# Hybrid encoder layer on one core: activations become the stationary matmul operand, split weights stream past them 512 columns at a time

## The chip, the cores and the metric

One core of a Trainium2 chip runs the whole program in one launch. The metric is the device time of that launch in microseconds. Before the change it is 2490.61 us, the median of 3 runs (2490.39 to 2492.17). Everything is float32 in HBM.

## What is computed

256 tokens of width 2048 go through one encoder layer. Cut to what matters:

```python
x = x + 0.5 * swiglu_ffn(rms_norm(x), w_gate, w_up, w_down)     # 2048 -> 5632 -> 2048
h = rms_norm(x)
u = h @ w_in          # conv a, conv gate (2048 each), q latent 768, kv latent 512, k rope 64, two gates of 2048
y_conv = silu(layer_norm(depthwise_conv31(a * sigmoid(gate)) + b)) @ w_pw_out
y_mla  = attention(16 heads: q from (rms_norm(c_q) @ w_uq), k and v from (rms_norm(c_kv) @ w_ukv), rope) @ w_o
x = x + (sigmoid(gl_conv) * y_conv + sigmoid(gl_mla) * y_mla) @ w_out
x = x + 0.5 * swiglu_ffn(rms_norm(x), w_gate2, w_up2, w_down2)
return rms_norm(x)
```

The weights are read once from HBM (427 MB read over the span). With 256 tokens the arithmetic lies almost wholly in the products with weights.

## The kernel before

**Split products.** A float32 product is made of three passes in the type fp32r: each weight tile is rounded by ACT into `w_hi` (`round_unit`, line 332, a Copy), DVE writes the remainder `w_lo = raw - w_hi` (`split_unit`, line 780), and the activations are kept as a rounded half and a remainder too (`h`, `hidden`, `attn`, `merged`, `c_q`, `c_kv`: 256 columns of high part and 256 of low part for each tile of 128 channels). `multiply` issues the three matmuls:

```python
pe.matmul(dst[:, 0:T], w_hi[:, j, rows], moving[:, 0:T], start=start, stop=False)      # line 554
pe.matmul(dst[:, 0:T], w_hi[:, j, rows], moving[:, T:2 * T], start=False, stop=False)  # line 555
pe.matmul(dst[:, 0:T], w_lo[:, j, rows], moving[:, 0:T], start=False, stop=stop)       # line 556
```

The first operand after the destination is the stationary one: a 128x128 tile of weights is loaded into the array (LDWEIGHTS), and all 256 tokens (`T`) stream past it. So a result has channels on partitions and tokens along the row, which is the form in which the next product wants it.

**Units and slots.** The weights come as a stream of 760 units through four slots. SP's queue loads `raw[:, j]` once `lo_ready` tells that DVE is done with the slot (line 275), ACT rounds it once PE has used the slot four units earlier (`unit_used`), DVE splits it, PE multiplies. A unit is 128x1024 (8 weight tiles, 24 matmuls), in the two `down` stages 128x1408 (11 tiles, 33 matmuls), in two units of each head pair 128x1152.

**Stages**, in the order of PE's queue: ffn1_up, ffn1_down, conv_in, latents, heads (8 pairs), mla_out, conv_gate, conv_out, w_out, ffn2_up, ffn2_down. `over` makes hardware loops of equal groups. PE accumulates in two banks in turn and waits in `wait_bank` until DVE has read one (`tile_read`). DVE's and ACT's queues are written out by hand between the splits and roundings: `times` (line 814) reads a bank and applies the norm's factor, which lies along the tokens, `absorb` (lines 824 to 832) squares, rounds and splits a new tile of `x`, ACT takes the silu and the sigmoids (line 376, 385). The sums of squares are added tile by tile on DVE and summed over partitions by a matmul with ones (line 614), for which PE waits at the start of a stage. The convolution's 31 taps for each of 16 channel tiles run on DVE alone (`convolve`, line 958: one 128x256 instruction for each tap and tile), spread over conv_in, heads and mla_out. In heads, the scores (lines 670, 671), the transposes of the probabilities (line 679) and the product with the values (line 688) are full float32, and the rope swap is a matmul (line 727).

Of the kernel before, what the change touches and what calls it, by code (L numbers as in the profile page):

```python
# [14 lines left out]
P = 128  # L31
# [5 lines left out]
N_HEADS = 16  # L37
ROPE = 64
# [9 lines left out]
SLOTS = 4  # L48
UNIT_MAX = FT // 4


PHASES = [
    ("ffn1_up", FT, (8, 8, 8, 8), 2),
    ("ffn1_down", KT, (FT // 4,) * 4, 1),
    ("conv_in", KT, (8, 8, 8, 8), 2),
    ("latents", 6, (8, 8, 8, 8), 2),
    ("heads", N_HEADS // 2, (9, 9, 8, 8), 6),
    ("mla_out", KT, (8, 8, 8, 8), 2),
    ("conv_gate", KT // 2, (8, 8, 8, 8), 2),
    ("conv_out", KT // 2, (8, 8, 8, 8), 2),  # L60
    ("w_out", KT // 2, (8, 8, 8, 8), 2),
    ("ffn2_up", FT, (8, 8, 8, 8), 2),
    ("ffn2_down", KT, (FT // 4,) * 4, 1),
]


class Phase:
# [3 lines left out]
    def __init__(self, name, n, sizes, g0, t0):  # L71
        self.name, self.n, self.sizes, self.g0, self.t0 = name, n, sizes, g0, t0


def plan():

    out, group, tile = [], 0, 0
    for name, n, sizes, tiles in PHASES:
        out.append(Phase(name, n, sizes, group, tile))
        group += n  # L80
        tile += n * tiles
    return out


def encoder(nc, streams, x_in, pos_in, gains_in, conv_in, const_in, freq_in, out):
    phases = plan()
    ph = {p.name: p for p in phases}

    with ExitStack() as ctx:
# [5 lines left out]


        raw = sb("raw", [P, SLOTS, UNIT_MAX * P])
        w_hi = sb("w_hi", [P, SLOTS, UNIT_MAX * P], F32R)
        w_lo = sb("w_lo", [P, SLOTS, UNIT_MAX * P], F32R)
        x = sb("x", [P, KT, T])  # L100
        h = sb("h", [P, KT, 2 * T], F32R)
        consts = sb("consts", [P, 3 * P])
        identity, swap, ones = (consts[:, n * P:(n + 1) * P] for n in range(3))

        gains = sb("gains", [P, 6 * KT + QT + KVT, 1])
        taps = sb("taps", [P, KT, TAPS + 1])
        freq = sb("freq", [P, 2])
        rstd = sb("rstd", [P, T])
        rstd_q = sb("rstd_q", [P, T])
        rstd_kv = sb("rstd_kv", [P, T])  # L110
        rstd_kv_col = sb("rstd_kv_col", [P, 2])
        sum_sq = sb("sum_sq", [P, T])
        sq = sb("sq", [P, T])
        prod = sb("prod", [P, T])
        ta = sb("ta", [P, T])
        tb = sb("tb", [P, T])
        tcd = sb("tcd", [P, 2 * T])
        tc, td = tcd[:, 0:T], tcd[:, T:2 * T]
        small = sb("small", [P, 8])
        conv_acc = sb("conv_acc", [P, 2 * T])  # L120
        pos_i = sb("pos_i", [1, T], I32)
        trig = sb("trig", [P, 2 * T])
        sin, cos = trig[:, 0:T], trig[:, T:2 * T]
        angle, turns = conv_acc, tcd

        ln_gate = (conv_acc[:, 0:T], conv_acc[:, T:2 * T], sin, cos)
        mean = rstd_kv
        rstd_ln = rstd_q
        pos_f = td[0:1, :]

        ffn = ExitStack()
        hidden = sb("hidden", [P, FT, 2 * T], F32R, ffn)
        ffn.close()
        start = ExitStack()
        sb("before_x0", [P, FT * 2 * T - KT * T], F32, start)
        x0_sq = sb("x0_sq", [P, KT, T], F32, start)
        start.close()
# [4 lines left out]
        squares = sb("squares", [P, KT, T], F32, outs)  # L142
        tree = sb("tree", [P, KT // 2, T], F32, outs)
        outs.close()
        attn = sb("attn", [P, KT, 2 * T], F32R)
        outs = ExitStack()
        merged32 = sb("merged32", [P, KT, 2 * T], F32, outs)
        outs.close()
        outs = ExitStack()
        merged = sb("merged", [P, KT, 2 * T], F32R, outs)  # L150
        outs.close()
        c_kv = sb("c_kv", [P, KVT, 2 * T], F32R)
        c_q = sb("c_q", [P, QT, 2 * T], F32R)
        q_nope = sb("q_nope", [P, 2, T])
        q_rope = sb("q_rope", [P, T])
        k_nope = sb("k_nope", [P, 2, T])
        value = sb("value", [P, 2, 2 * P])
        probs = sb("probs", [P, 2, 2 * T])
        probs_t = sb("probs_t", [P, 2, 2 * T])
        row_max = sb("row_max", [P, 2, 2])  # L160
        row_sum = sb("row_sum", [P, 2, 2])
        row_inv = sb("row_inv", [P, 2, 2])
        rope_raw = sb("rope_raw", [P, T])
        k_rope = sb("k_rope", [P, T])
# [3 lines left out]
        for name, n in (("ffn1", KT), ("mix", KT), ("ffn2", KT), ("final", KT), ("ln_g", KT),  # L168
                        ("ln_b", KT), ("q", QT), ("kv", KVT)):
            gain[name] = gains[:, at:at + n, :]  # L170
            at += n

        bank = [ctx.enter_context(nc.psum_tensor(f"bank{n}", [P, 2 * T], F32)) for n in range(4)]
        scores = [ctx.enter_context(nc.psum_tensor(f"scores{n}", [P, 2 * T], F32)) for n in range(2)]
        turned0 = ctx.enter_context(nc.psum_tensor("turned0", [P, 2 * T], F32))
        misc = ctx.enter_context(nc.psum_tensor("misc", [P, 2 * T], F32))

        turned = (turned0, misc)


# [1149 lines left out]
```

## Time and profile before

| | |
|---|---|
| median of 3 runs | 2490.61 us |
| span of the profiled execution (first to last instruction) | 2489.8 us |
| median less span (what lies around it) | 0.8 us |
| PE busy | 2411.5 us, 97% |
| DVE busy, ACT busy | 1627.8 us, 1127.2 us |
| HBM read | 427.29 MB, 172 GB/s over the span |
| mean granted TensorE clock | 0.990 |

The profiled execution's own time is given by its span; the launch time of that same execution is not listed apart. A row of the trace names the line, the engine, the operation, output and inputs, the shape and the count; then busy time and mean duration of one, and the idle time ahead of it with what ended it. Matmuls are pipelined, so the duration of one (some 280 ns) is longer than the distance from one start to the next; what PE costs is read from the starts.

### The profile page before, as it was taken

How to read it: one execution, taken by the hardware profiler on the slowest of the kernel's cores; microseconds unless marked ns; L12 is line 12 of the kernel's file. 1: busy time of each engine (PE TensorE's matmuls, PEld its weight loads, DVE VectorE, ACT ScalarE, POOL GpSimd, SP SyncE). 2: the span in 40 equal slices, each digit the busy share in tenths (PEclk: the TensorE clock that was granted, in tenths of full speed). 3: DMA queues.
4: the chain of work that ended last, by engine and by line, in shares of the span. 5: the costliest groups of instructions: out<-in, count | busy, mean ns of one | idle time of the engine just before them, and what ended most of it. 6: DMA issues, size and time to landing. Idle time of an engine off the chain costs nothing.

```text
span 2489.8 us, 51907 instructions
## 1 busy us (share of the span) xinstructions
PE 2411.5 (97%) x19734; PEld 2379.9 (96%) x19734; DVE 1627.8 (65%) x2441; ACT 1127.2 (45%) x1227; POOL 16.2 (1%) x12
## 2 busy tenths in 40 slices
PE   6999999999999999989999998999999999999997
PEld 6999999999999999977799998999999999999997
DVE  6655556565555778799967777677555555554444
ACT  5555554543334454345443355334555455543332
POOL 2000000000000000000000000000000000000000
PEclk9999999999999999999999999999999999999998
DMA  5555555565554555422255545555555555565552
GB/s 194 185 180 183 182 181 185 180 206 186 185 185 154 179 187 181 160 91 97 92 170 185 179 159 160 185 184 177 179 185 180 182 185 178 185 201 187 185 186 102
DMA packets 111215, 430.03 MB, mean 173 GB/s; under 512 B 12609, under 2 KB 12738, under 8 KB 111170
## 3 DMA queue, kind: packets, MB, share of 16 engines
q1 hardware_dynamic: 111170, 429.43, 51.9%
q8 instruction: 28, 0.46, 0.1%
q14 instruction: 17, 0.14, 0.0%
HBM read 427.29 MB, written 2.10 MB: 172 GB/s over the span
## 4 chain that ended last, share of the span: by engine, by line
PE 88%; DVE 8%; issue 2%; ACT 2%; DVEq 0%; DMA 0%; ACTq 0%; SPq 0%
PE bank L556 29%; PE bank L554 29%; PE bank L555 29%; DVE conv_acc L958 2%; DVE w_lo L780 2%; ACT w_hi L332 1%; DVE h L872 1%; DVE row_inv L1029 0%; DVE tree L1119 0%; ACT probs L401 0%; PE scores L688 0%; DVE x L1204 0%; PE misc L679 0%; PE misc L614 0%; DVE padded L1136 0%
## 5 line engine op out<-in xcount | busy, mean ns | idle before, releaser
L780 DVE TENSOR_TENSOR w_lo<-raw,w_hi 128x1024 fp32r<-128x1024 f32 (+2 forms) x760 | 985.1, 1297 | 785.1 <-ACT w_hi L332 773.2
L332 ACT ACTIVATE w_hi<-raw 128x1024 fp32r<-128x1024 f32 (+2 forms) x760 | 846.9, 1115 | 1179.3 <-PE bank L556 1170.4
L554 PE MATMUL bank<-h,w_hi 128*128 128x256 f32 x4032 | 1145.4, 284 | 29.8 <-DVE h L872 23.1
L555 PE MATMUL bank<-h,w_hi 128*128 128x256 f32 x4032 | 1143.0, 283 | 0.0
L556 PE MATMUL bank<-h,w_lo 128*128 128x256 f32 x4032 | 1142.9, 283 | 0.0
L554 PEld LDWEIGHTS bank<-h,w_hi 128*128 128x128 f32 x4032 | 776.1, 192 | 32.0 <-issue 24.3
L555 PEld LDWEIGHTS bank<-h,w_hi 128*128 128x128 f32 x4032 | 776.1, 192 | 0.2
L556 PEld LDWEIGHTS bank<-h,w_lo 128*128 128x128 f32 x4032 | 776.1, 192 | 0.0
L556 PE MATMUL bank<-hidden,w_lo 128*128 128x256 f32 x1408 | 395.6, 281 | 0.0
L554 PE MATMUL bank<-hidden,w_hi 128*128 128x256 f32 x1408 | 394.2, 280 | 0.0
L555 PE MATMUL bank<-hidden,w_hi 128*128 128x256 f32 x1408 | 391.4, 278 | 0.0
L554 PEld LDWEIGHTS bank<-hidden,w_hi 128*128 128x128 f32 x1408 | 264.7, 188 | 0.0
L555 PEld LDWEIGHTS bank<-hidden,w_hi 128*128 128x128 f32 x1408 | 264.7, 188 | 0.0
L556 PEld LDWEIGHTS bank<-hidden,w_lo 128*128 128x128 f32 x1408 | 264.3, 188 | 0.0
L958 DVE SCALAR_TENSOR_TENSOR conv_acc<-padded,taps,conv_acc 128x256 f32<-128x256 f32 x464 | 188.3, 477 | 0.0
L554 PE MATMUL bank<-attn,w_hi 128*128 128x256 f32 x512 | 144.1, 281 | 2.9 <-DVE attn L1043 1.5
L555 PE MATMUL bank<-attn,w_hi 128*128 128x256 f32 x512 | 143.5, 280 | 0.0
L556 PE MATMUL bank<-attn,w_lo 128*128 128x256 f32 x512 | 143.5, 280 | 0.0
L376 ACT ACT_TABLE_LOAD x84 | 107.8, 1283 | 1.5
L554 PEld LDWEIGHTS bank<-attn,w_hi 128*128 128x128 f32 x512 | 96.5, 188 | 3.4 <-DVE attn L1043 1.8
L555 PEld LDWEIGHTS bank<-attn,w_hi 128*128 128x128 f32 x512 | 96.5, 188 | 0.0
L556 PEld LDWEIGHTS bank<-attn,w_lo 128*128 128x128 f32 x512 | 96.4, 188 | 0.0
(163 smaller groups left out, 1632.1 us busy)
## 6 DMA issues: line engine op xcount, KB each, us to landing
raw<-in_ffn_up SPq DMA_DIRECT2D x352, 512.0 KB, 3.3
raw<-in_ffn_down SPq DMA_DIRECT2D x128, 704.0 KB, 4.0
raw<-in_conv_in SPq DMA_DIRECT2D x64, 512.0 KB, 3.3
raw<-in_mla_out SPq DMA_DIRECT2D x64, 512.0 KB, 3.4
raw<-in_conv_gate SPq DMA_DIRECT2D x32, 512.0 KB, 3.7
raw<-in_conv_out SPq DMA_DIRECT2D x32, 512.0 KB, 3.3
raw<-in_w_out SPq DMA_DIRECT2D x32, 512.0 KB, 3.3
raw<-in_latents SPq DMA_DIRECT2D x24, 512.0 KB, 3.5
```

Source lines behind the costliest of these rows:

```text
L332: act.activation(w_hi[:, j, 0:n], raw[:, j, 0:n], ACT.Copy).then_inc(hi_ready, 1)
L376: act.activation(tb[:, :], ta[:, :], ACT.Silu).then_inc(gate_active, 1)
L554: pe.matmul(dst[:, 0:T], w_hi[:, j, rows], moving[:, 0:T], start=start, stop=False)
L555: pe.matmul(dst[:, 0:T], w_hi[:, j, rows], moving[:, T:2 * T], start=False, stop=False)
L556: return pe.matmul(dst[:, 0:T], w_lo[:, j, rows], moving[:, 0:T], start=False, stop=stop)
L780: dve.tensor_tensor(w_lo[:, j, 0:n], raw[:, j, 0:n], w_hi[:, j, 0:n], ALU.subtract).then_inc(lo_ready, 1)
L872: dve.scalar_tensor_tensor(out=h[:, m, T:2 * T], in0=x[:, m, :], scalar=gain["ffn1"][:, m, :], in1=h[:, m, 0:T], op0=ALU.mult, op1=ALU.sub ...
L958: dve.scalar_tensor_tensor(out=acc, in0=src, scalar=weight, in1=acc, op0=ALU.mult, op1=ALU.add).then_inc(tap_done, 1)
```

## The change

Nearly every product is turned round. The stationary operand is now 128 channels by 128 tokens of activations, two token halves `tt` for each channel tile, and the split weights stream past it 512 columns wide (`WIDE`). A result is 128 tokens by 512 channels and fills a whole bank; a group of columns takes two banks. A unit is 128x1024: two channel tiles deep (`DEEP`) and 512 wide, 12 matmuls; there are 814 units and still four slots.

```diff
-                pe.matmul(dst[:, 0:T], w_hi[:, j, rows], moving[:, 0:T], start=start, stop=False)
-                pe.matmul(dst[:, 0:T], w_hi[:, j, rows], moving[:, T:2 * T], start=False, stop=False)
-                return pe.matmul(dst[:, 0:T], w_lo[:, j, rows], moving[:, 0:T], start=False, stop=stop)
+                pe.matmul(dst, fixed_hi, moving_hi, start=first, stop=False)
+                pe.matmul(dst, fixed_hi, moving_lo, start=False, stop=False)
+                return pe.matmul(dst, fixed_lo, moving_hi, start=False, stop=last)
...
+            def wide_unit(u, g):
+                fixed = STATIONARY[g.stage]
...
+                for r in range(DEEP):
+                    k = DEEP * (u - g.u0) + r
+                    moving = w_hi[:, slot, r * w:(r + 1) * w], w_lo[:, slot, r * w:(r + 1) * w]
+                    for tt in range(2):
+                        tokens = slice(tt * P, (tt + 1) * P)
+                        last = multiply(banks(g)[tt][:, 0:w], (fixed[:, k, 0, tokens], fixed[:, k, 1, tokens]), moving,
+                                        k == 0, k == g.deep - 1)
+                last.then_inc(unit_used, 1)
...
+            def turn(n, src, first_column):
+
+                if n > 1:
+                    pe.wait_ge(*turn_freed(n - 2))
+                for r in range(2):
+                    for tt in range(2):
+                        c = first_column + r * P
+                        last = pe.transpose(turned_bank[n % 2][:, r * T + tt * P:r * T + (tt + 1) * P],
+                                            src[:, tt, c:c + P], identity[:, :])
+                last.then_inc(turned, 1)
...
-                    else:
-                        dve.wait_ge(tap_done, done + (t - 1))
-                        dve.scalar_tensor_tensor(out=acc, in0=src, scalar=weight, in1=acc,
-                                                 op0=ALU.mult, op1=ALU.add).then_inc(tap_done, 1)
+                if by_scalar(t):
+                    made = taps_made(n) // 4 - 1 - (i + 1)
+                    dve.wait_ge(tap_made, taps_made(n))
+                    dve.wait_ge(tap_done, taps_done(n - 1))
+                    dst = conv[:, 4 * i:4 * i + 4, :] if t == TAPS - 1 else conv_acc
+                    dve.tensor_tensor(dst, conv_acc, conv_prod[made % 2], ALU.add).then_inc(tap_done, 1)
+                    return
```

- A result that feeds a product must have channels on partitions again, so it is transposed by PE in blocks of 128x128, four to a `turn` (470 transposes in all, 64 of which are the probabilities' and were there before), then copied (and rounded) by ACT and split by DVE (`take_turns`). `TURNS` and `TURN_AFTER` set how many turns a group has and after which later unit PE does them: two units later, four and five for the latents.
- The norm's factor is now one number for each token, that is for each partition. It is applied as the scale of the instruction that reads the bank. Sums of squares come from ACT's `accum_out`, and the matmuls with ones are gone, as is GpSimd's part at the start.
- In heads, query and key products keep the weights stationary (256 columns moving), and the rope part of the queries is a stage of its own before heads. `k_rope` is laid out with zeros to 128 rows, so that the rope part of the scores runs over 128 rows instead of 64. The two gate products run ahead of heads.
- The 31 taps are shared: for 21 of them ACT makes the products for four channel tiles (84 instructions for a block of four tiles) and DVE adds 128x1024 at once; for 10 of them DVE does four 128x256 instructions as before. `taps_due` spreads them at 0.85 tap a unit from the 22nd unit of conv_in to the end of the gates (130 units), the last 14 beside the first head pairs. The layer norm of the channels is done token by channel: transposed by `fore` during mla_out, centred and scaled, and transposed back by `back`.
- All loops are written out: no hardware loop is left.

PE's queue. `turned` is the bank of transposes, `prod` the gated product of a group. Before, a piece of ffn1_up's loop:

```order
L556 MATMUL bank<-h,w_lo 128x256
L559 ISA [waits tile_read]
L554 MATMUL bank<-h,w_hi 128x256 [waits lo_ready]
L555 MATMUL bank<-h,w_hi 128x256
L556 MATMUL bank<-h,w_lo 128x256
```

After, the end of the second unit that follows the first finished group of ffn1_up:

```order
L661 MATMUL bank<-w_hi,h 128x512
L662 MATMUL bank<-w_lo,h 128x512
L663 MATMUL bank<-w_hi,h 128x512
L672 MATMUL turned<-identity,prod 128x128 [waits by_dve]
L672 MATMUL turned<-identity,prod 128x128 x7
L661 MATMUL bank<-w_hi,h 128x512 [waits lo_ready]
```

The matmuls are half as many and twice as wide, and eight transposes that wait for DVE's product stand between two units.

DVE's queue beside the taps. Before, a group of conv_in:

```order
L780 TENSOR_TENSOR w_lo<-raw,w_hi 128x1024 [waits hi_ready,tile_read]
L958 SCALAR_TENSOR_TENSOR conv_acc<-padded,taps,conv_acc 128x256 [waits tap_done,glu_ready]
L958 SCALAR_TENSOR_TENSOR conv_acc<-padded,taps,conv_acc 128x256 [waits tap_done] x7
L780 TENSOR_TENSOR w_lo<-raw,w_hi 128x1024 [waits hi_ready]
L814 TENSOR_TENSOR tcd<-bank,rstd 128x256 [waits unit_used]
```

After, at the gates, where `q_rope` names the store that holds the accumulator and ACT's products:

```order
L900 TENSOR_TENSOR w_lo<-raw,w_hi 128x1024 [waits hi_ready]
L1083 TENSOR_TENSOR q_rope<-q_rope 128x4x256 [waits tap_done,tap_made]
L1089 SCALAR_TENSOR_TENSOR q_rope<-padded,taps,q_rope 128x256 [waits tap_done,tap_made]
L1089 SCALAR_TENSOR_TENSOR q_rope<-padded,taps,q_rope 128x256 x3
```

What was a row of eight tap instructions between two splits is now one wide add, or four narrow instructions, and both wait for products that ACT makes one unit ahead.

SP's queue at the start. After (before, the four pairs of loads of `x` and `raw` were followed at once by the constants, and PE's first matmul waited for neither):

```order
L397 DMA x<-in_x_in 128x4096
L394 DMA xt<-in_xt_in 128x512
L390 DMA raw<-in_ffn_up 128x1024 [waits lo_ready]
L398 DMA identity<-in_const_in 128x128
L399 DMA taps<-in_taps_in 128x512
```

The input is loaded twice, transposed (`xt`, eight loads) and plain (`x`), and the constants, for which PE's first matmul now waits (`small_loaded`), come behind the eighth load of weights, which waits until four units are split.

## Rows read from the trace of the kernel before

**Rows 1.** Page: busy time of each engine over the span.
```profile
PE 2411.5 (97%) x19734; PEld 2379.9 (96%) x19734; DVE 1627.8 (65%) x2441; ACT 1127.2 (45%) x1227; POOL 16.2 (1%) x12
```
**Rows 2.** Stretches: from:to, length, PE, PEld, DVE, ACT, POOL busy (count), clock, DMA share, GB/s.
```profile
28.80:515.00 486.20, 486.20 (x4048) 485.68 (x4046) 288.26 (x386) 251.63 (x255) 0.00 (x0) 1.00 0.54 182
515.00:725.00 210.00, 210.00 (x1783) 210.00 (x1782) 119.95 (x138) 76.66 (x59) 0.00 (x0) 1.00 0.58 191
...
1030.00:1240.00 210.00, 188.82 (x1201) 162.05 (x1200) 196.82 (x436) 93.56 (x183) 0.00 (x0) 0.93 0.30 99
```
**Rows 3.** PE in order of time, ffn1_up: start us, us, engine, instruction.
```profile
500.00 0.28 PE L554 MATMUL bank<-h,w_hi 128*128 128x256 f32 x1
500.00 0.19 PEld L555 LDWEIGHTS bank<-h,w_hi 128*128 128x128 f32 x1
500.12 0.28 PE L555 MATMUL bank<-h,w_hi 128*128 128x256 f32 x1
```
**Rows 4.** PE in order of time, heads.
```profile
1150.20 0.41 PE L554 MATMUL bank<-c_kv,w_hi 128*128 128x256 f32 x1
1150.41 0.41 PE L555 MATMUL bank<-c_kv,w_hi 128*128 128x256 f32 x1
```
**Rows 5.** The stretch round rows 4, columns as in rows 2.
```profile
1149.00:1151.40 2.40, 2.40 (x13) 2.40 (x12) 2.24 (x5) 1.61 (x3) 0.00 (x0) 0.50 0.62 221
```
**Rows 6.** PE in order of time, the float32 work of heads.
```profile
1153.86 1.89 PE L688 MATMUL scores<-probs_t,value 128*128 128x256 f32 x8
...
1158.98 0.70 PE L671 MATMUL scores<-k_rope,q_rope 64*128 64x256 f32 x2
1159.61 0.70 PE L670 MATMUL scores<-k_nope,q_nope 128*128 128x256 f32 x2
...
1196.47 0.66 PE L679 MATMUL misc<-consts,probs 128*128 128x128 f32 x4
1196.88 0.36 PE L554 MATMUL bank<-c_kv,w_hi 128*128 128x256 f32 x1
1197.08 0.28 PE L555 MATMUL bank<-c_kv,w_hi 128*128 128x256 f32 x1
```
**Rows 7.** Waits of PE: engine, line, releaser, us in total, times, longest.
```profile
PE bank L554 <- DVE h L872: 23.1, 1, 23.1
PE turned L679 <- ACT probs L401: 15.4, 8, 2.8
PE misc L614 <- DVE sum_sq L832: 8.6, 4, 4.0
```
**Rows 8.** Groups of DVE and ACT by shape: count, busy us, mean ns, idle before.
```profile
L780 DVE TENSOR_TENSOR w_lo<-raw,w_hi 128x1024 fp32r<-128x1024 f32 x616 | 755.4, 1227 | 558.0 <-ACT w_hi L332 548.2 <-DVE sum_sq L832 2.8 <-DVE merged L814 1.0
L1029 DVE TENSOR_REDUCE row_inv<-scores 128x2 f32<-128x512 f32 x16 | 11.0, 686 | 0.0
...
L332 ACT ACTIVATE w_hi<-raw 128x1024 fp32r<-128x1024 f32 x616 | 651.5, 1058 | 859.2 <-PE bank L556 850.3
...
L407 ACT ACTIVATE probs_t<-misc 128x512 f32<-128x512 f32 x8 | 4.6, 580 | 0.0
```
**Rows 9.** DVE in order of time, conv_in.
```profile
860.96 1.23 DVE L780 TENSOR_TENSOR w_lo<-raw,w_hi 128x1024 fp32r<-128x1024 f32 x1 [1.56 <-ACT w_hi L332]
862.10 0.42 DVE L814 TENSOR_TENSOR ta<-bank,rstd 128x256 f32<-128x256 f32 x1
...
864.98 3.25 DVE L958 SCALAR_TENSOR_TENSOR conv_acc<-padded,taps,conv_acc 128x256 f32<-128x256 f32 x8
```
**Rows 10.** Stretches of the start, columns as in rows 2.
```profile
0.00:5.00 5.00, 0.00 (x0) 0.00 (x0) 0.00 (x0) 0.00 (x0) 0.20 (x4) 1.00 0.55 147
...
10.00:15.00 5.00, 0.00 (x0) 0.00 (x0) 5.00 (x3) 5.00 (x11) 4.84 (x4) 1.00 1.00 397
```
**Rows 11.** The end, in order of time.
```profile
2473.30 0.28 PE L556 MATMUL bank<-hidden,w_lo 128*128 128x256 f32 x1
...
2482.06 5.08 SPq L296 DMA_DIRECT2D out<-x  x4
```

More of the change, by code:

```diff
@@ L37 @@
 N_HEADS = 16
+PAIRS = N_HEADS // 2
 ROPE = 64
@@ L47 @@
 EPS = 1e-6
+WIDE = 512
+DEEP = 2
 SLOTS = 4
[L49 to L64, printed above, removed]
@@ L67 @@
[L67 to L87, printed above, removed]
+UNIT = WIDE * DEEP
@@ L89, in encoder @@
+def encoder(nc, streams, xt_in, x_in, pos_in, gains_in, final_in, taps_in, const_in, freq_in, out):
+    plan = Plan()
+    groups, turns, units = plan.groups, plan.turns, plan.units
+    n_units = len(units)
+    H0 = plan.heads
+    M0 = plan.at("mla_out")
     with ExitStack() as ctx:
@@ L170, in encoder @@
             gain[name] = gains[:, at:at + n, :]
             at += n
[L173 to L178, printed above, removed]
-        raw_loaded = [sem(f"raw_loaded{j}") for j in range(SLOTS)]
+        bank = [ctx.enter_context(nc.psum_tensor(f"bank{n}", [P, WIDE], F32)) for n in range(6)]
@@ L531, in _ @@
-            for j in range(3):
-                round_unit(ph["mla_out"], 2, j)
-            rounds(ph["mla_out"], ph["conv_gate"], mla_out_work, 1)
-            gates = ph["conv_gate"]
-            for j in range(3):
-                round_unit(gates, 1, j)
-            for g in range(LN_AT):
-                gate_group(g, beside={CENTRE_AT: square, LN_AT - 1: lambda n: root() if n == 1 else None}.get(g))
-            over(act, LN_AT, gates.n - 2, ln_group)
-            ln_group(gates.n - 2)
-            gate_group(gates.n - 1)
@@ L643, in _ @@
-            over(pe, 1, KT, two_tiles(ph["conv_in"], h))
-            latents = ph["latents"]
-            for g in range(latents.n):
-                two_tiles(latents, h)(g)
-                if g == 2:
-                    pe.wait_ge(summed, KT + KVT)
-                    total(sum_sq[:, :])
-                    for tt in range(2):
-                        last = pe.matmul(misc[:, T + tt:T + tt + 1], sum_sq[:, tt * P:(tt + 1) * P], ones[:, 0:1],
-                                         start=True, stop=True)
-                    last.then_inc(total_ready, 1)
@@ L804, in rounds @@
-            def rounds(phase, following, work, step=1, start=0, mid=None):
-                def body(g, r, i):
-                    group(phase, following, work, g, r, i, mid)
-                over(dve, start, phase.n - 1, body, step)
-                body(phase.n - 1, (phase.n - 1) % step, (phase.n - 1) // step)
-            def times(dst, src, factor, tile, complete):
-                dve.wait_ge(*complete)
-                dve.tensor_tensor(dst, src[:, 0:T], factor, ALU.mult).then_inc(tile_read, 1)
-                dve.wait_ge(tile_read, tile + 1)
@@ new lines, in _ @@
+            g = groups[-1]
+            finish(plan.ends[n_units - 1])
+            variance("final", 4, D)
+            for tt in range(2):
+                part_of_x = x[:, tt, columns_of(g)]
+                dve.tensor_tensor(part_of_x, part_of_x, final_gain[:, columns_of(g)], ALU.mult).then_inc(gained, 1)
+            factor("final", rstd)
+            dve.wait_ge(gained, 8)
+            for n in range(4):
+                part_of_x = x[:, 0, WIDE * n:WIDE * (n + 1)]
+                dve.tensor_scalar(part_of_x, part_of_x, rstd[:, 0:1], None, ALU.mult).then_inc(out_by_dve, 1)
```

1759 lines of the change are left out of this document (924 added, 835 removed).

## The prediction

> **What bounds the kernel now.** I read the page's engine totals first, then busy time by stretches, then PE's instructions in order of time, and last its waits. The totals put PE in front: it is busy 97% of the span, DVE 65%, ACT 45% [rows 1]. By stretches it is busy without a gap in the feed-forward stages [rows 2]: 4048 matmuls in 486.2 us is one each 120.1 ns, and 1783 in 210 us one each 117.8 ns. Only heads has holes, with PE 188.8 us of 210 and the clock at 0.93. So nearly all of the time is the number of matmuls times the distance between them, and that distance has to be understood. In order of time the starts stand 0.12 us apart, and the load of the next weights starts together with each matmul [rows 3]. The same instruction at a clock of 0.50 (1.2 GHz) has starts 0.213 us apart [rows 4, 5], which is one cycle a column (256/1.2 = 213.3 ns) and nothing on top. At the full 2.4 GHz 256 columns would be 106.7 ns, but 118 to 120 pass. Something of 118 to 120 ns goes with each matmul, and it is covered once the columns take longer than that.
>
> **What 512 columns cost.** The nearest row is the float32 product with the values: each record streams 256 columns at two cycles each, so 512 cycles, with a load of weights of its own, at full clock. Eight records take 1.89 us from first start to last end; less one duration (mean 379 ns) and over seven that is 0.216 us apart [rows 6]. I take **215.8 ns** for a 512-column matmul. Bounds: 213.3 ns below (the columns alone, as at half clock), 2 x 119.7 = 239.4 ns above (nothing gained for a column). Cited by itself: the Trainium skill, TensorE: Matmul & The Clock Gate, section Back-to-back issue gap, gives for a stream of loads and matmuls a sustained 131 ns at 512 columns; taken for true, the 9288 wide matmuls below would take 1217 us, and the kernel some 1460 us.
>
> **PE's work after the change.** Counts come from its queue.
> - 9288 matmuls of 512 columns x 0.2158 = 2004.4 us. They replace 18,576 of 256 columns, at 0.1197 some 2223 us. This is the gain: 219 us.
> - 96 of 320 columns: 320/2.4 + 2.5 (the same 2.5 above the columns as in 215.8) = 135.8 ns, 13.0 us.
> - 672 of 256 columns left in heads x 0.118 = 79.3 us.
> - Scores: 128 records. Now they stand 0.313 us apart (two in 0.63 us) [rows 6]. The product with the values, of the same shape but over 128 rows all through, has 0.216. The rope part had 64 rows and gets 128. I take 0.216, 27.6 us, as nearest in form; if the 0.313 stays it is 40.1.
> - Values: 64 records x 0.216 = 13.8 us.
> - 470 transposes. At full clock four of them and the change back take 1196.88 - 1196.47 = 0.41 us, and the next matmul comes 0.20 later instead of 0.12 [rows 6]: about 0.49 us for four, of which 4 x 0.109 is the transposes and 0.06 the change. 470 x 0.109 + 75 changes x 0.06 = 51.2 + 4.5 = 55.7 us. Of it 406 transposes, 44 us, are new.
>
> Sum: 2193.8 us.
>
> **Before and behind it.**
> - Start: PE now starts at 23.1 us [rows 7]. After, it waits for constants behind 8 x 0.79 MB of transposed input and weights, 2.1 MB of plain input and 0.35 MB of the rest, 8.7 MB. The loads of the start move 0.74 MB in the first 5 us and 397 GB/s after [rows 10], so they begin in effect at 3.1 us, and that is 3.1 + 8.7/0.39 = 25.4, say 25.5 us. The loads' waits for splits don't bind: a unit costs ACT two 128x256 and one rounding, under 2.1 us, about as long as its 0.79 MB take to land. The first 5.7 us at half clock, as now, lose 2.9 us.
> - End: now 16.5 us lie between the last matmul at 2473.3 and 2489.8 [rows 11]. After, the factor's chain runs on 2 columns rather than 256 and needs no matmul; the scaling is shared by ACT and DVE. Two bank reads of 0.69, the squares, a chain of some eight small instructions, four scalings and the last store; with 0.2 to 0.3 us for a small one and 0.6 for a scaling, both estimates by the 0.58 and 0.69 of 512 columns [rows 8], and 3 us for the store (four take 5.1 us in all [rows 11]), some 11 us.
>
> **What the other engines do beside it.** Twelve matmuls are 2.59 us a unit. A rounding costs ACT 1.06 us and a split costs DVE 1.14 us from start to start [rows 8, 9], so the feed-forward stages stay PE's, with an ACT share of some 20 and a DVE share of some 22 in 42 us of a gate and an up group (16 units, two or four instructions of 0.6 to 0.7, and the copies). A unit is 0.52 MB in 2.59 us, 202 GB/s against 397 shown at the start [rows 10]. The wait before the transposes costs nothing: DVE has two units, 5.2 us, for two reads of 0.69 (the reduction of 128x512 took 0.686 [rows 8]); if that cover were gone, each of 22 up groups would cost up to 1.4 us.
> The taps are the tight place. One block of four tiles costs DVE 20 adds of 1.14 and 10 x 4 instructions of 0.40 (eight in 3.25 us [rows 9]), 38.8 us for 31 taps, 1.25 a tap. At 0.85 tap a unit DVE has 1.14 + 1.06 = 2.20 us a unit against PE's 2.59; ACT has 1.06 + 0.85 x 84 x 0.4/31 = 1.98 (0.4 is an estimate for 128x256; the straight line through 1058 ns for 1024 and 580 for 512 columns [rows 8] gives 0.34). In the latents DVE also has some 13 us of factors, scalings and splits over 24 units: 63 us there against PE's 58. I put **5 us** of waits there. In the layer norm of the channels, ACT takes four squares of two instructions of 0.6 to 0.8 us between roundings, then a root, and DVE the factor before `back` can start; counted from the end of unit 15 of mla_out the scaled columns come at some 17 us, and PE is there at 13: **5 us**. Other joints of stages: **7 us**. Heads: the transposes of the probabilities wait 2.0 us a pair now (15.4 us in 8 [rows 7]), and the clock drops after them [rows 5]. After, a whole pair's products (16 us) lie between the scores and their transposes, and the wait is gone, as are the waits for sums (8.6 us [rows 7]).
>
> Sum: 25.5 + 2.9 + 2193.8 + 17 + 11 = 2250 us of span; the median stood 0.8 us above the span, so **2252 us** in round numbers, against a profiled span of 2489.8: 9.6% less.
>
> **A rule against the trace.** The starts show 118 to 120 ns at full clock and 213 at half clock, where a cost on top of the columns would give more than 213 [rows 3, 4]. By the same page of the Trainium skill, section LDWEIGHTS, a load of 128 columns takes 128/1.2 = 107 ns whatever the rows are. By this rule the load would be the floor under each matmul and 512 columns would cover it (the 2252 us); the trace agrees as far as the floor goes, though it stands 11 to 13 ns above the rule's figure.
>
> **Rivals.**
> - *A cost for each matmul on top of its columns*: 120 - 106.7 = 13 ns rather than 2.5. Then 226.4 ns, 9288 x 10.6 = 98 us more: **2350 us**. For it: the 13 ns are there in each row. Against: nothing of it at half clock, nor among the transposes, which have the same 106.7 ns of array time and a load each and stand 0.109 apart.
> - *DVE sets the pace beside the taps*: each step now waits on ACT's product and on the step before it. If that adds 0.5 us net to each of 146 units, 73 us: **2325 us**. For it: DVE is busy 196.8 of 210 us in heads now [rows 2], where it has taps; against: a split always stands between two taps and covers the latency.
> - *The change doesn't do what it says*: the chip streams this type at 119.7 ns for 256 columns however they are cut. 9288 x 23.6 ns = 219 us more: **2471 us**, still under the time before. Against it: the 213 ns at half clock leave no such rate visible, and no row at full clock excludes it for fp32r.
> - *The sustained 131 ns a wide matmul*: 2250 - 787 = **1463 us**. It would stream 3.9 columns a ns, where the fastest row has 256 in 118 ns, 2.2 a ns.
> - *Slower, by the clock*: PE waits a little for DVE or ACT in every unit from conv_in to heads, and the granted clock falls to 0.50 as it does in heads now after a wait of 2 us [rows 5, 7]. A unit at half clock is 5.18 us, 2.59 more. To be slower by over 0.2% it takes 2496 - 2252 = 244 us, that is 94 of the 152 units between the first tap and heads; all of them give 2252 + 394 = **2646 us**. Against it: no row shows the clock down after short waits, and DVE has 0.4 us to spare in each unit.
>
> **How the numbers follow.** 0.2%, about 5 us, is what a measurement of this kernel can tell from no change. Chances: forecast 0.72, DVE's pace 0.13, cost for each matmul 0.07, no gain for a column 0.04, sustained 131 ns 0.01, slower by the clock 0.03. The forecast's own range is 2215 to 2300: 213.3 instead of 215.8 ns takes 23 us off, no waits 17 us; the scores at 0.313 add 12, waits twice or three times as long 17 to 34. The range of 8 in 10 reaches over the two next cases, to 2360. Faster by over 0.2%: all but the last case and a little of the 2471: 0.96; within: 0.01; slower: 0.03.
>
> **What would show it.** Wide matmuls with starts 0.216 us apart in the feed-forward stages and PE busy there without a gap; 0.226 or 0.239 would be the first or the third rival. Transposes 0.11 apart, scores 0.216 apart. PE's first matmul near 25.5 us. In the gates, DVE some 2.2 us busy of each 2.6; PE waiting there for `w_lo` in total over 20 us would be the second rival, a granted clock under 0.9 the last. Behind PE's last matmul 11 us. The prediction is wrong if the distance of the wide matmuls isn't 0.213 to 0.218, or if PE's idle time behind its start is over 50 us.

## The result, and the profile after

The changed kernel takes **2375.44 us**, the median of 4 runs (2374.88 to 2376.26), against 2490.64 us before; the ratio is 0.9539, with a 95% interval of 0.9525 to 0.9552. It is 115 us faster, where 239 were forecast, and lies 15 us above 2360 us, the upper end of the stated range.

The page of the profile after: the span, the busy time of each engine, the chain that ended last, and the groups of the matmuls (line, engine, operation, operands, count | busy, mean ns of one | idle before and what ended it).

```profile
span 2373.1 us, 26781 instructions
...
PE 2319.3 (98%) x10718; PEld 1926.1 (81%) x10718; DVE 1322.5 (56%) x1469; ACT 1188.6 (50%) x1619; POOL 0.2 (0%) x4
...
PE 96%; DVE 2%; issue 1%; ACT 1%; DMA 1%; SPq 0%; ACTq 0%; DVEq 0%
...
L661 PE MATMUL bank<-w_hi,h 128*128 128x512 f32 (+1 forms) x2144 | 836.3, 390 | 28.0 <-DMA pos_i<-in_pos_in 26.4
...
L661 PE MATMUL bank<-w_hi,hidden 128*128 128x512 f32 x704 | 278.8, 396 | 0.0
```

Beside [rows 1], PE has 9016 matmuls fewer and is still busy 98% of the span. DVE has 305 us less. So the kernel is bound by PE as before, and the time is again the number of matmuls times the distance between them. That distance is read from PE in order of time. In h's stage:

```profile
100.03 0.39 PE L661 MATMUL bank<-w_hi,h 128*128 128x512 f32 x1
100.25 0.39 PE L662 MATMUL bank<-w_lo,h 128*128 128x512 f32 x1
100.48 0.39 PE L663 MATMUL bank<-w_hi,h 128*128 128x512 f32 x1
100.71 0.39 PE L661 MATMUL bank<-w_hi,h 128*128 128x512 f32 x1
```

Three steps take 0.68 us, **0.227 us each and not 0.216**. It is clearer over more of them. A row of one line's group gives count, shortest, median and longest duration in ns, and the first and the last start. Here for h (137 to 155 us) and for hidden (598 to 615 us):

```profile
L661 PE MATMUL bank<-w_hi,h x27: 389/389/389, 137.0 to 154.7; 128*128 128x512 f32 x27
```
```profile
L661 PE MATMUL bank<-w_hi,hidden x25: 395/396/396, 597.7 to 614.5; 128*128 128x512 f32 x25
```

Each of these is one matmul of three, so the first has 26 x 3 = 78 steps in 17.7 us, 0.2269 us, and the second 24 x 3 = 72 steps in 16.8 us, **0.2333 us**. The same instruction, with the same shape, is 6.5 ns slower when it reads `hidden`. Over all starts of a stage the means are 226.8 ns for h (6336 matmuls), 233.3 for hidden (2112), and 233.3 to 233.6 for attn, merged and c_q (840). These means, and those below, leave out the few distances behind a wait, beside transposes or at half clock.

What PE waited for, in total, times and the longest:

```profile
PE bank L661 <- DMA pos_i<-in_pos_in: 26.4, 1, 26.4
PE turned L672 <- DVE c_q L1038: 8.5, 1, 8.5
PE bank L773 <- issue: 1.7, 1, 1.7
PE bank L661 <- DVE w_lo L900: 1.5, 2, 1.1
PE turned L672 <- DVE conv_tok L1130: 1.5, 1, 1.5
PE bank L773 <- DVE q_nope L1110: 0.9, 1, 0.9
```

Beside [rows 7] the waits of heads for turned probabilities and for sums are gone. One wait of 8.5 us is new, and it costs more than itself. PE stood idle from 1020.1 us, and the granted clock fell to 0.50 from 1023.6 us on. The stretch behind the wait, columns as in [rows 2], and matmuls in it, which stand 0.43 us apart:

```profile
1028.50:1033.80 5.30, 5.24 (x16) 4.30 (x17) 1.67 (x5) 3.55 (x8) 0.00 (x0) 0.50 0.35 104
...
1030.33 0.63 PE L662 MATMUL bank<-w_lo,h 128*128 128x512 f32 x1
1030.76 0.63 PE L663 MATMUL bank<-w_hi,h 128*128 128x512 f32 x1
1031.18 0.63 PE L661 MATMUL bank<-w_hi,h 128*128 128x512 f32 x1
```

Against the distances at full clock these 5.3 us of work lose some 2.5 us. Stretches of two places, columns as in [rows 2]: conv_in with the gates, and heads.

```profile
800.00:1010.00 210.00, 210.00 (x981) 176.47 (x981) 169.97 (x216) 152.75 (x261) 0.00 (x0) 1.00 0.60 186
...
1210.00:1335.00 125.00, 122.36 (x899) 117.78 (x898) 77.39 (x128) 90.88 (x199) 0.00 (x0) 1.00 0.40 123
```

Beside the taps PE has no gap in 210 us, with DVE at 81% and ACT at 73%. In heads the granted clock is 1.00, where it was 0.93 in [rows 2], and PE is idle 2.6 us of 125.

### The profile page after: what moved, and what is told of

Same layout as the page of the kernel before. It is cut to its first block, busy times and chain, and to the rows that moved or that the text cites. A ratio compares the mean times of both kernels' runs of the same rounds, so it can differ in the third digit from the quotient of the medians.

```text
span 2373.1 us, 26781 instructions
## 1 busy us (share of the span) xinstructions
PE 2319.3 (98%) x10718; PEld 1926.1 (81%) x10718; DVE 1322.5 (56%) x1469; ACT 1188.6 (50%) x1619; POOL 0.2 (0%) x4
## 4 chain that ended last, share of the span: by engine, by line
PE 96%; DVE 2%; issue 1%; ACT 1%; DMA 1%; SPq 0%; ACTq 0%; DVEq 0%
PE bank L663 31%; PE bank L662 31%; PE bank L661 31%; PE turned L672 2%; PE bank L799 1%; PE bank L773 1%; PE bank L774 1%; DMA pos_i<-in_pos_in 0%; DVE q_rope L1083 0%; DVE w_lo L900 0%; ACT w_hi L422 0%; DVE q_rope L1089 0%; PE turned L784 0%; DMA raw<-in_ffn_up 0%; PE turned L853 0%
## 5 line engine op out<-in xcount | busy, mean ns | idle before, releaser
L661 PE MATMUL bank<-w_hi,h 128*128 128x512 f32 (+1 forms) x2144 | 836.3, 390 | 28.0 <-DMA pos_i<-in_pos_in 26.4
L663 PE MATMUL bank<-w_hi,h 128*128 128x512 f32 (+1 forms) x2144 | 833.4, 389 | 0.0
L662 PE MATMUL bank<-w_lo,h 128*128 128x512 f32 (+1 forms) x2144 | 833.2, 389 | 0.0
L661 PEld LDWEIGHTS bank<-w_hi,h 128*128 128x128 f32 x2144 | 403.7, 188 | 110.8 <-DMA pos_i<-in_pos_in 26.4
L663 PEld LDWEIGHTS bank<-w_hi,h 128*128 128x128 f32 x2144 | 403.3, 188 | 82.7
L662 PEld LDWEIGHTS bank<-w_lo,h 128*128 128x128 f32 x2144 | 403.5, 188 | 81.6
L661 PE MATMUL bank<-w_hi,hidden 128*128 128x512 f32 x704 | 278.8, 396 | 0.0
L662 PE MATMUL bank<-w_lo,hidden 128*128 128x512 f32 x704 | 278.4, 395 | 0.0
L663 PE MATMUL bank<-w_hi,hidden 128*128 128x512 f32 x704 | 278.4, 395 | 0.0
L663 PEld LDWEIGHTS bank<-w_hi,hidden 128*128 128x128 f32 x704 | 132.2, 188 | 31.9
L661 PEld LDWEIGHTS bank<-w_hi,hidden 128*128 128x128 f32 x704 | 132.3, 188 | 31.9
L662 PEld LDWEIGHTS bank<-w_lo,hidden 128*128 128x128 f32 x704 | 132.3, 188 | 31.8
L524 ACT ACTIVATE q_rope<-padded,taps 128x256 f32<-128x256 f32 x320 | 135.7, 497 | 1.0 <-DVE q_rope L1083 1.0
L661 PE MATMUL bank<-w_hi,attn 128*128 128x512 f32 x128 | 52.4, 410 | 0.0
L663 PE MATMUL bank<-w_hi,attn 128*128 128x512 f32 x128 | 50.8, 397 | 0.0
```

Source lines behind the costliest of these rows:

```text
L524: act.activation(conv_prod[made % 2][:, r, :], padded[:, m, t:t + T], ACT.Copy, scale=taps[:, m, t:t + 1]).then_inc(tap_made, 1)
L661: pe.matmul(dst, fixed_hi, moving_hi, start=first, stop=False)
L662: pe.matmul(dst, fixed_hi, moving_lo, start=False, stop=False)
L663: return pe.matmul(dst, fixed_lo, moving_hi, start=False, stop=last)
```

## The experiments

Two things stood open: what the 11 ns above 215.8 belong to, and why the stages other than h's pay 6.5 ns more. Then come the smaller terms of the sum.

### Is it the number of matmuls? Each 512 columns as two of 256 (e4)

```diff
-                        last = multiply(banks(g)[tt][:, 0:w], (fixed[:, k, 0, tokens], fixed[:, k, 1, tokens]), moving,
-                                        k == 0, k == g.deep - 1)
+                        for lo, hi in ((0, T), (T, w)):
+                            last = multiply(banks(g)[tt][:, lo:hi], (fixed[:, k, 0, tokens], fixed[:, k, 1, tokens]),
+                                            (moving[0][:, lo:hi], moving[1][:, lo:hi]), k == 0 and lo == 0, k == g.deep - 1 and hi == w)
```

> The changed kernel with each wide matmul of 512 columns issued as two of 256 with the same stationary operand, so twice the matmuls and loads of weights and the same columns. Theory A (13.3 ns belongs to each fp32r matmul whatever its columns): 18,576 matmuls at 120 ns and more, 240 instead of 228.8 for a pair, 9288 x 11 = 100 us more, 2478 us, and PE's distances are 120 in the stages of h. Rival E (the type streams 6% slower for each column): nothing changes, 2375 us, distances 113.4 ns. Rival F (the load of weights is the floor at 256 columns, over 120 ns): more than 2480 us.

Measured: 2475.11 us, 0.994 of before (0.9923 to 0.9957). The group of one line in h's stage, 137 to 155 us:

```profile
L661 PE MATMUL bank<-w_hi,h x51: 283/283/283, 137.0 to 155.0; 128*128 128x256 f32 x51
```

150 steps in 18.0 us are 0.120 us. With 226.8 for 512 columns and 120.0 for 256, a column costs 106.8/256 = 0.417 ns, which is 2.4 columns a ns, and in h's stage **some 13.4 ns are left over for each matmul, whatever its width**. The 96 matmuls of 320 columns fit: 133.3 + 13.4 = 146.7, and the starts stand 146 and 147 ns apart. So the load of the next weights is not a floor of 120 ns under the columns. It, or something that goes with it, comes on top.

### Is it the type? bfloat16 in place of fp32r (e6)

The type of the split stores is changed, and a padding of 16 KB a partition is put behind `merged`; as the stores are half as large, the distances between them change too. The halves then keep fewer bits, so the product is less exact. The number and the shapes of all instructions are the same.

```diff
-F32R = mybir.dt.float32r
+F32R = mybir.dt.bfloat16
```

> The changed kernel with every fp32r store (w_hi, w_lo, h, hidden, attn, merged, c_kv, c_q) in bfloat16: the same matmuls and loads, operands half as wide, so the result is less exact. Theory G (what stands above 213.3 ns comes of reading 4-byte operands): wide matmuls at 216 ns, in heads under 118 ns, 2250 us or less. Rival A (it belongs to each pair of load and matmul of any type): 226.7 ns, 2350 us.

Measured: **2255.16 us**, 0.9055 of before (0.9037 to 0.9073). The group in h's stage, 137 to 155 us, and the page's loads of weights of this kernel and of the changed one:

```profile
L662 PE MATMUL bank<-w_hi,h x28: 379/379/379, 137.2 to 154.7; 128*128 128x512 bf16 x28
...
L662 PEld LDWEIGHTS bank<-w_hi,h 128*128 128x128 bf16 x2144 | 210.1, 98 | 279.9 <-DMA pos_i<-in_pos_in 26.6
```
```profile
L661 PEld LDWEIGHTS bank<-w_hi,h 128*128 128x128 f32 x2144 | 403.7, 188 | 110.8 <-DMA pos_i<-in_pos_in 26.4
```

81 steps in 17.5 us are 0.216 us, in every stage alike. The forecast's price of a wide matmul is there once the operands are bfloat16, and the time is 3 us from the forecast. That the time comes so near is in part luck: the 672 matmuls of 256 columns took 109 ns for the 118 forecast (6 us less) and the changes to transposes and back some 4 us less, while PE waited 20 us for 17, worked some 3 us longer for half clock behind those waits, and the end took 3 us more. So the term that was badly out is the price of the fp32r matmul. The 13.4 ns aren't a matter of four bytes alone: the full float32 work of heads, in the changed kernel itself, has no such part. Its scores, start and duration:

```profile
1236.85 0.59 PE L774 MATMUL bank<-k_rope,q_rope 128*128 128x256 f32 x2
1237.28 0.59 PE L773 MATMUL bank<-k_nope,q_nope 128*128 128x256 f32 x2
1237.71 0.59 PE L774 MATMUL bank<-k_rope,q_rope 128*128 128x256 f32 x2
```

Two in 0.43 us are 0.216 each, for 256 columns at two cycles. The recorded load is 188 ns for fp32r and 98 ns for bfloat16. Whether the load or the stream carries the 13.4 ns stays open: no kernel with operands of two types was tried.

The Trainium skill, TensorE: Matmul & The Clock Gate, section Back-to-back issue gap, gives N/2.4 + 2.5 ns for a matmul by itself at full clock. The rows of bfloat16 agree with that to the nanosecond (216, 136 and 109 for 512, 320 and 256 columns). They don't agree with the sustained 131 ns that the same section gives for 512 columns. For fp32r the runs show some 13.4 in place of 2.5.

### Why hidden pays 6.5 ns more: addresses (e1, e2, e3, e5, e8)

`hidden`, `attn`, `merged` and `c_q` start at an odd multiple of 32 bytes in the changed kernel, h at a multiple of 64. In e1, 32 bytes ahead of `hidden` bring all of them to multiples of 64:

```diff
+        sb("shift_hidden", [P, 8])
         outs = ExitStack()
         hidden = sb("hidden", [P, FT, 2, T], F32R, outs)
```

> The changed kernel with 32 bytes of padding before the store of hidden, so that hidden, attn, merged and c_q, the stationary operands whose wide matmuls stood 232 to 237 ns apart, begin on a multiple of 64 bytes as h does (226.7 ns). Theory A (the start address of the stationary operand costs the 6.6 ns): 2952 wide matmuls fall to 226.7 ns, 19.5 us less, 2356 us. Rival B (the stage costs it: its length, its turns, what DVE and ACT do beside it): distances stay at 233.3, 2375 us.

Measured: 2370.74 us, 0.9521 (0.9505 to 0.9537): 4.7 us less than the changed kernel, and neither the near 20 that alignment was to bring nor the unchanged time of the rival. attn, merged and c_q fell to about 229 ns. hidden did not move (598 to 615 us):

```profile
L662 PE MATMUL bank<-w_hi,hidden x25: 393/393/398, 597.9 to 614.7; 128*128 128x512 f32 x25
```

In e2 the weights were moved as well, by 32 bytes, with the stationary stores kept on multiples of 64:

```diff
+        sb("shift_weights", [P, 8])
         w_hi = sb("w_hi", [P, SLOTS, UNIT], F32R)
...
+        sb("shift_x", [P, 8])
         x = sb("x", [P, 2, D])
...
+        sb("shift_hidden", [P, 8])
```

> As e1, and w_hi and w_lo, the moving operands, begin 32 bytes off a multiple of 64, all stationary ones on it. In the kernel before, hidden was moving and 32 off, and its matmuls of 256 columns stood 117.7 ns apart instead of 120. Theory A (a moving operand that is off shortens the 13.3 ns by some 2.3): 224.4 ns, 9288 x 2.3 = 21 us under e1, 2335 us. Rival B (an operand that is off costs 6.6 ns whichever it is): 233.3 ns, 2417 us. Rival C: no effect at 512 columns, as e1, 2356 us.

Measured: **2416.84 us**, 0.9704 (0.9688 to 0.972), 46 us more than e1, which is rival B's number. h is now slow too (137 to 155 us), 75 steps in 17.5 us, 0.2333:

```profile
L664 PE MATMUL bank<-w_hi,h x26: 395/396/396, 137.1 to 154.6; 128*128 128x512 f32 x26
```

And in e3 the weights moved with all that lies behind them, so that both operands of h are off 64 and keep their distance (the same edit without `shift_x`):

> The changed kernel with both stationary and moving operands of all wide matmuls 32 bytes off a multiple of 64. Theory A (what counts is each operand's own address): the stationary one's 6.6 ns is there in all stages, less what e2 shows for the moving one; with e2's theory 231 ns, 9288 x 231 against 9288 x 228.8 now, 2395 us. Rival D (what counts is the distance between the two addresses): equal offsets give 226.7 ns everywhere, 2356 us as e1.

Measured: 2370.89 us, 0.9522 (0.9506 to 0.9538). h is fast again, 81 steps in 18.4 us, which ends rival B. The 2356 us of rival D didn't come, since hidden went only from a distance of 32 to 64 bytes and stayed at 233.3:

```profile
L663 PE MATMUL bank<-w_hi,h x28: 389/389/389, 136.6 to 155.0; 128*128 128x512 f32 x28
```

So h is fast with both operands off 64 bytes and slow with one: neither operand's own alignment decides. What counts is **how far apart the streamed and the stationary operand lie**. The next kernel, e5, put each stage at a distance of its own, by paddings of 256, 352, 320, 384 and 320 bytes ahead of the five stores (`shift_h` and so on, as above):

> The changed kernel with padding in front of each stationary store, so that the distance of its first byte from the weights' store, modulo 512 bytes, is 256 for h, 128 for hidden, 320 for attn, 384 for merged and 192 for c_q. Known so far: 0 gives 226.7 ns between wide matmuls, 32, 64 and 416 give 233.3, 448 gives 229. Theory D (the two reads meet in the store, and the distance of their addresses decides): five different distances in time, some of them under 226.7 ns; if h at 256 stands at 216 ns, 6336 x 10.7 = 68 us less, 2307 us. Rival A (0 is the best there is, 13.3 ns belongs to the matmul): no stage under 226 ns, all others near 233, and with h at 233.3 the time is 2375 + 42 = 2417 us.

Measured: 2372.25 us, 0.9524 (0.9508 to 0.954). No stage came under 226 ns, as rival A had it, but h at 256 stayed fast, which rival A had not. The slots, channel tiles and halves of all these stores are multiples of 512 bytes, so one number describes a stage: the start of the stationary store less that of `w_hi`, modulo 512. The mean distance of starts over the stage, from five kernels:

| distance modulo 512 B | ns between starts | stage and kernel |
|---|---|---|
| 0 | 226.8 | h in the changed kernel and in e3 |
| 256 | 226.8 | h in e5 |
| 192 | 228.9 | c_q in e5 |
| 448 | 228.9 to 229.4 | attn, merged, c_q in e1 |
| 480 | 233.0 to 233.4 | attn, merged, c_q in e2 |
| 128 | 232.4 | hidden in e5 |
| 384 | 232.6 | merged in e5 |
| 32 | 233.3 | hidden in the changed kernel, h in e2 |
| 64 | 233.3 | hidden in e1 and e3 |
| 320 | 233.3 | attn in e5 |
| 416 | 233.3 to 233.6 | attn, merged, c_q in the changed kernel |
| 96 | 234.3 | hidden in e2 |

One store, h, was fast at two distances and slow at a third, with the same work beside it. The test that remained was to bring all of them to 0, in e8:

```diff
+        sb("shift_hidden", [P, 120])
...
+        sb("shift_attn", [P, 32], F32, outs)
...
+        sb("shift_merged", [P, 32])
```

> Theory D (the distance between the streamed and the stationary operand's addresses, modulo 512 bytes, sets the part above 226.8 ns): with every stationary buffer a multiple of 512 bytes from w_hi, all wide matmuls stand 226.8 ns apart, hidden's too (233.3 in the changed kernel). 2112 x 6.5 + 840 x 6.4 = 19 us less: about 2356 us. Rival (the stage does it: other streams, banks or engines beside it, and h is the fast one for that): hidden stays at 233.3 and the time at 2371 or above.

Measured: **2358.81 us**, 0.9471 (0.9455 to 0.9487), 16.6 us less than the changed kernel. hidden, 598 to 615 us:

```profile
L664 PE MATMUL bank<-w_hi,hidden x25: 389/389/389, 598.2 to 614.5; 128*128 128x512 f32 x25
```

72 steps in 16.3 us, 0.2264; over the whole stage it is 226.7, the same as h; merged has 226.9 and c_q 227.3. The distance theory holds and the stage theory falls. Of the 2.4 us short of the expected 19, three parts are seen. attn's mean stays at 228.4 ns, which is 0.6 us and isn't explained. The 672 matmuls of 256 columns in heads went from 119 to 120 ns, as 0 is a bad distance at that width (in e4 too: h at 0 has 120.0, hidden at 32 has 118.4). And the granted clock fell once more than in the changed kernel, behind a wait of 1.9 us for transposes of `conv_tok`, which loses some 1.5 us:

```profile
1398.80:1402.20 3.40, 3.40 (x11) 2.81 (x11) 3.40 (x7) 1.40 (x3) 0.00 (x0) 0.50 0.18 74
```

At 256 columns the kernel before had thus shown the distance the other way round, and by little: 120.1 ns for h and 117.8 for hidden [rows 2].

The Trainium skill, SBUF — State Buffer, section Who interferes with whom, gives the PE two read ports, one for the moving operand and one for loading weights, and calls them independent. Here a shift of 32 bytes between the two costs 6.5 ns in each matmul, so at fp32r what a matmul costs hangs on both addresses together. Where the two operands meet, no run shows.

### The price of the transposes (e7)

```diff
-                for r in range(2):
+                for r in (0, 1, 0, 1):
```

> The changed kernel with every transpose of the turns issued twice (372 more transposes of 128x128, same result). My price: 372 x 0.109 = 40.6 us more, 2416 us. Rival: the transposes hide in waits or cost a change of mode each, 2375 us or over 2440 us.

Measured: 2415.65 us, 0.9699 (0.968 to 0.9718). 372 transposes more cost 40.2 us, 0.108 us each, and nothing but themselves. The forecast had 0.109. So the 406 new transposes are, by this price, 44 us of the changed kernel in PE's queue.

### The start (e9)

```diff
-            sp.dma_start(identity[:, :], const_in).then_inc(small_loaded, 16)
...
                 if u == 3:
+                    sp.dma_start(identity[:, :], const_in).then_inc(small_loaded, 16)
...
             def turn_group(n):
                 g = groups[n]
+                if g.turn == 0:
+                    pe.wait_ge(small_loaded, 64)
...
-            pe.wait_ge(small_loaded, 64)
             u = 0
```

The other three constants move with the first.

> The constants are loaded before x, behind the fourth pair of input and weights, and TensorE waits for them only at its first transposes. If its start at 26.4 us is set by the last of these constants as the wait shows, it now starts when the first columns of h and of the weights are there and the rest keeps ahead of it: 10 to 14 us less, 2361 to 2365 us. Rival: the first units wait one by one for their own loads and splits instead, and little is won: 2372 us or more.

Measured: **2358.51 us**, 0.9471 (0.9455 to 0.9487), 16.9 us less than the changed kernel and more than expected. PE's waits for weights, and its first matmuls:

```profile
PE bank L661 <- DVE w_lo L901: 11.8, 4, 8.8
...
8.84 0.80 PE L661 MATMUL bank<-w_hi,h 128*128 128x512 f32 x1 [8.84 <-DVE w_lo L901]
9.43 0.63 PE L662 MATMUL bank<-w_lo,h 128*128 128x512 f32 x1
9.86 0.63 PE L663 MATMUL bank<-w_hi,h 128*128 128x512 f32 x1
```

PE starts 17.6 us earlier. Of the three short waits, 3.0 us in all, two (1.5 us) lie shortly before the wait of 8.5 us and are in the changed kernel too, so PE gives back 1.5 us, in one wait at 21.9 us while loads still come in. The remaining 0.8 us is of the size of what a shorter stretch of half clock behind the 8.5 us wait saves: 6.8 us here, 10.2 us in the changed kernel.

### The wait of 8.5 us (e10)

PE waits there for a bank of transposes to be freed. DVE in order of time shows why it is late, start and duration:

```profile
1021.96 1.21 DVE L900 TENSOR_TENSOR w_lo<-raw,w_hi 128x1024 fp32r<-128x1024 f32 x1
1023.10 1.22 DVE L1083 TENSOR_TENSOR q_rope<-q_rope 128x1024 f32<-128x1024 f32 x1
1024.23 1.22 DVE L900 TENSOR_TENSOR w_lo<-raw,w_hi 128x1024 fp32r<-128x1024 f32 x1
1025.37 1.22 DVE L1083 TENSOR_TENSOR padded<-q_rope 128x1024 f32<-128x1024 f32 x1
1026.51 1.21 DVE L900 TENSOR_TENSOR w_lo<-raw,w_hi 128x1024 fp32r<-128x1024 f32 x1
1027.64 1.65 DVE L1038 SCALAR_TENSOR_TENSOR c_q<-turned,gains,c_q 128x256 fp32r<-128x256 f32 x4
```

Three turns of the queries' latent fall due at one unit, with two banks. The third can start only when DVE has split the first, and three splits and the taps stand ahead of that in DVE's queue. The experiment turns the third, and the keys with it, four units later, in all three queues:

```diff
                 for b in range(g.turns):
+                    if g.kind == "q1" and late != (b == 2):
+                        continue
...
+                if u == Q_END + 9:
+                    turn_group(plan.ends[Q_END], True)
```

> The third pair of query columns, and the keys' turned part with it, are turned four units later than the first two pairs. If the 8.5 us before the transposes of c_q are DVE's scaling of the last group that came due at once with them, the wait is gone: about 8 us less, 2367 us. Rival: the same wait comes back behind the first two pairs, or one unit on: 2375 us.

Measured: **2365.37 us**, 0.9498 (0.9482 to 0.9514), 10.1 us less. The wait on `c_q` is gone from the list, which now begins:

```profile
PE bank L665 <- DMA pos_i<-in_pos_in: 26.7, 1, 26.7
PE bank L665 <- DVE w_lo L908: 1.9, 3, 1.1
PE bank L779 <- issue: 1.7, 1, 1.7
```

It brings more than the expected 8 us because the granted clock no longer falls there: it is 1.00 from 1000 to 1060 us. The wait of 8.5 us and the 2.5 us of half clock are 11 us; a start 0.3 us later and 0.4 us more of waits for `w_lo` take back most of the difference.

### All three (e11)

> All three at once. If the savings lie at different places of the chain they add up: 19 + 12 + 8 = 39 us less, about 2337 us. Rival: they overlap, or the earlier start is eaten by a later wait: over 2345 us.

Measured: **2331.03 us** (2330.73 to 2332.15), 0.9362 of before (0.9346 to 0.9377). That is 44.4 us less than the changed kernel, and the three by themselves are 16.6 + 16.9 + 10.1 = 43.6. They lie at different places of one chain, so they add, to within 1 us. This kernel, with only stores, loads and turns moved, beats both.

## Why the prediction was wrong in size

The direction and the bound were right, and so was that a matmul of 512 columns costs less than two of 256. The reason given, that what goes with each matmul is covered once the columns take longer, was wrong. **The step that failed is the first term of the sum, 9288 x 0.2158.** With the measured distances:

| term | forecast | measured | us more |
|---|---|---|---|
| wide matmuls | 9288 x 215.8 ns | 6336 x 226.8, 2112 x 233.3, 840 x 233.3 | 70 + 37 + 15 = 122 |
| 320 columns | 135.8 ns | 146.6 ns | 1 |
| 256 columns in heads | 118 ns | 119 ns | 1 |
| scores, values, transposes | 0.216, 0.216, 0.109 us | the same | 0 |
| changes to transposes and back | 4.5 us | about 0.7 us | -4 |
| start | 25.5 us | 26.4 us | 1 |
| half clock at the start | 2.9 us | about 2 us | -1 |
| half clock behind the 8.5 us wait | none | about 2.5 us | 3 |
| waits | 17 us | 14.1 us | -3 |
| behind PE's last start | 11 us | 13.6 us | 3 |
| span | 2250 | 2373.1 | 123 in all; the terms give 123 |

The 0.7 us is what the distances beside the transposes have above the usual ones: the first wide matmul starts 28 ns behind the last transpose, where 109 ns is usual, and the next one 314 ns behind it, where 227 is, so little remains of the 0.06 us forecast for a change.

The wide matmuls' excess falls into two. The larger, 11.0 ns in each of 9288, is 102 us. That is the rival "a cost for each matmul on top of its columns", which gave 226.4 ns and 2350 us and had a chance of only 0.07. The smaller, 6.5 ns in 2952 of them, is 19 us, and no term stood for it. The prediction had read 120.1 ns for one stage and 117.8 for another [rows 2], the same effect at 256 columns, and asked nothing of the difference.

Two arguments had spoken against that rival, the half clock and the full float32 work, and both were weaker than they looked.
- *Nothing at half clock.* That is true, also at 512 columns: the starts at a granted clock of 0.50 shown above, at 1030.33 us and behind, stand 0.43 us apart, and 512/1.2 = 426.7 ns is the columns alone. So do PE's third to fifth starts, though the clock column has no reading below 1.00 there:

```profile
27.46 0.63 PE L663 MATMUL bank<-w_hi,h 128*128 128x512 f32 x1
27.89 0.63 PE L661 MATMUL bank<-w_hi,h 128*128 128x512 f32 x1
28.32 0.63 PE L662 MATMUL bank<-w_lo,h 128*128 128x512 f32 x1
```

  A cost on top of the columns at 2.4 GHz need not be there at 1.2 GHz. The forecast took one level as evidence for the other.
- *The float32 records have 0.216, and the transposes, which the prediction named, 0.109.* Both are full float32, another type, at two cycles a column. I took them as "nearest in form", by cycles and loads; nearest in type were the rows of 118 to 120 themselves, and these show 13 ns. Where two nearest rows disagree and the difference times 9288 is 100 us, 0.07 is too little for the second.

The starts of e4 and of the changed kernel show no floor: with 256 as with 512 columns some 13.4 ns come on top of the columns. The prediction had weighed a rule of the Trainium skill (TensorE: Matmul & The Clock Gate, section LDWEIGHTS, 128/1.2 = 107 ns for a load) as such a floor, which 512 columns would cover; the trace doesn't agree with that use of it.

The rest, point by point. Wide matmuls at 0.216: wrong, at 0.227 and 0.233. Transposes 0.109 and scores 0.216: right. PE's first matmul near 25.5 us: right within 1 us, and its cause was the named one, the constants behind the loads. DVE's pace beside the taps: not binding, as forecast; PE waits for `w_lo` only 1.5 us in all, so the rival of DVE's pace (2325 us) fell, though it lay nearer to the result than the forecast. The rival without gain for a column (2471 us) fell, since a 512-column matmul is 13 ns cheaper than two of 256, and so did 131 ns a matmul. The clock stayed at 1.00 in heads. The waits came to 14 us for 17, but that is luck: the latents' 5 us were put down to DVE's total work, and what came was one wait of 8.5 us on the order of its queue, with the half clock behind it. Behind PE's last start came 13.6 us for 11; the last instructions of ACT and DVE and the store there take as long as told, but the two reads of the bank by DVE stand in one row of 1.29 us, ACT's squares (two of 0.63 and 0.61, with two of 0.19 between and behind) wait for them, and ACT then loads a table, which was not in the sum:

```profile
2359.89 1.29 DVE L953 SCALAR_TENSOR_TENSOR x<-bank,x 128x512 f32<-128x512 f32 x2 [8.82 <-PE bank L663]
...
2361.97 1.28 ACT L426 ACT_TABLE_LOAD   x1
```

## What to carry to other kernels

Widening the streamed operand from 256 to 512 columns pays, though by the fixed part alone: with fp32r the 240.0 ns of two matmuls become 226.8, some 5.5%, not 10%. Find that fixed part from two widths of the same type at the same clock, never from another type or from half clock. Where PE is the bound, try the distance between the stores of the two operands, a few bytes of padding: here it was worth 17 us in one direction and cost 46 in the other. Then look at what PE's first matmul really waits for, and for transposes that fall due together with fewer banks than turns; a wait of PE can cost more than its length, by the half clock behind it (2.5 us on 8.5 here).

## What the runs showed of the hardware that was not expected

- At full clock and with the operands at distance 0, an fp32r matmul costs its columns at 2.4 a ns plus some 13.4 ns, at 256, 320 and 512 columns alike (120.0, 146.6 and 226.8 ns); bfloat16 has 2.5 ns in the same places, and float32 at two cycles a column about the same 2.5. At half clock (starts 0.43 us apart for 512 columns) fp32r shows nothing on top.
- The distance between the two operands in SBUF, modulo 512 bytes, moves an fp32r matmul of 512 columns between 226.8 ns (0 and 256) and 234.3 ns (96). At 256 columns it goes the other way round: 120 at 0, and in heads, where the weights are the stationary operand, 116 to 117 with c_q and c_kv 448 behind the weights (e1). In bfloat16 every stage had 216, at distances that weren't laid out on purpose.
- PE's first matmuls ran at half clock in both places where PE began: starts 0.43 us apart up to 30.4 us where it began at 26.45, and up to 12.9 us where it began at 8.84 (e9).
- In the changed kernel the granted clock fell to 0.50 at 1023.6 us, with PE idle since 1020.1, and came back at 1033.9, 5.3 us after PE had begun again. Without that wait (e10) it stayed at 1.00.
